# The first layer's first four modulation units: two channel tiles of shift and scale in each, and loads reordered to match

## What is computed

```python
c_act = silu(c)
for l in range(2):
    mod = c_act @ w_ada[l] + b_ada[l]                       # 6 * 1024 columns
    sh_mix, sc_mix, gt_mix, sh_mlp, sc_mlp, gt_mlp = split(mod, 6)
    h = rms_norm(x, g_pre_mix[l]) * (1 + sc_mix) + sh_mix
    y = mixer(h, w_in[l], ...)                              # u = h @ w_in first
    x = x + gt_mix * rms_norm(y, g_post_mix[l])
    ...
```

## Time and profile before

| | |
|---|---|
| three runs | 2279.96, 2281.36 (median), 2281.94 us |
| span of the profiled execution | 2274.4 us; its own run time is not among the numbers |
| mean granted TensorE clock | 0.994 of full speed |
| busy in the span | PE 2222.0 us (98%), DVE 1280.8 (56%), ACT 992.0 (44%), POOL 1131.6 (50%) |
| DMA, 0 to 80 us | 22.82 MB, mean 285 GB/s |
| DMA, whole span | 240.39 MB, mean 106 GB/s |

### The profile page before, as it was taken

How to read it: one execution, slowest core, us unless ns; L and a number is a source line. 1 busy time by engine, 2 the same in 40 slices (tenths; PEclk the granted TensorE clock), 3 DMA queues, 4 the chain that set the end, 5 groups by cost and what they waited for, 6 DMA issues and landing times.

```text
span 2274.4 us, 28727 instructions
## 1 busy us (share of the span) xinstructions
PE 2222.0 (98%) x10450; PEld 1749.5 (77%) x10450; DVE 1280.8 (56%) x2061; ACT 992.0 (44%) x1630; POOL 1131.6 (50%) x596
## 2 busy tenths in 40 slices
PE   8999999999999999999999999999999999999998
PEld 5886667788888878766778888887767688888886
DVE  4999847863546699984365122157776653221222
ACT  4368543333232335875344223244666653331323
POOL 2698833554444639876374344463422244444442
PEclk9999999999999999999999999999999999999999
DMA  8432205354646323221122323232222122333332
GB/s 319 138 98 71 65 29 172 120 185 157 231 166 217 96 77 94 75 84 38 56 84 86 99 93 101 87 108 72 82 57 65 47 92 94 103 92 97 97 99 86
DMA packets 206662, 240.39 MB, mean 106 GB/s; under 512 B 9762, under 2 KB 172378, under 8 KB 206554
## 3 DMA queue, kind: packets, MB, share of 16 engines
q1 hardware_dynamic: 205990, 238.76, 32.9%
q10 hardware_dynamic: 564, 0.21, 0.0%
HBM read 236.84 MB, written 2.10 MB: 105 GB/s over the span
## 4 chain that ended last, share of the span: by engine, by line
PE 52%; DVE 3%; POOL 2%; issue 2%; ACT 1%; DMA 0%; DVEq 0%; POOLq 0%; ACTq 0%; SPq 0%
PE product L2508 16%; PE product L2510 15%; PE product L2509 15%; DVE side L1888 1%; PE side L3076 1%; POOL ring_low L950 1%; PE product L3111 1%; POOL slot_f L981 1%; PE side L3096 1%; POOL slot_f L1003 1%; PE product L2881 1%; PE side L2865 0%; PE side L3023 0%; DVE slot_f L1888 0%; ACT sqt L1436 0%
## 5 line engine op out<-in xcount | busy, mean ns | idle before, releaser
L950 POOL TENSOR_TENSOR ring_low<-ring_f,ring_high 128x1024 fp32r<-128x1024 f32 (+1 forms) x349 | 845.6, 2427 | 1029.2 <-ACT ring_high L1076 1028.8
L2508 PE MATMUL product<-slot_r,ring_high 128*128 128x512 f32 (+1 forms) x2536 | 1007.1, 397 | 13.5 <-ACT slot_f L1282 4.0
L2510 PE MATMUL product<-slot_r,ring_high 128*128 128x512 f32 (+1 forms) x2536 | 989.3, 390 | 0.0
L2509 PE MATMUL product<-slot_r,ring_low 128*128 128x512 f32 (+1 forms) x2536 | 988.3, 390 | 0.0
L1076 ACT ACTIVATE ring_high<-ring_f 128x1024 fp32r<-128x1024 f32 (+1 forms) x349 | 367.8, 1056 | 697.9 <-DMA ring_f<-in_w_ff 326.0
L2508 PEld LDWEIGHTS product<-slot_r,ring_high 128*128 128x128 f32 (+1 forms) x2536 | 475.9, 188 | 146.4 <-issue 35.5
L2510 PEld LDWEIGHTS product<-slot_r,ring_high 128*128 128x128 f32 (+1 forms) x2536 | 475.9, 188 | 101.5
L2509 PEld LDWEIGHTS product<-slot_r,ring_low 128*128 128x128 f32 (+1 forms) x2536 | 476.4, 188 | 97.0 <-issue 1.4
L1845 DVE SCALAR_TENSOR_TENSOR va<-product,sqt 128x512 f32<-128x512 f32 x96 | 66.3, 692 | 332.9 <-ACT sqt L1154 331.6
L1888 DVE SCALAR_TENSOR_TENSOR side<-slot_f,cols,side 128x512 f32<-128x512 f32 x322 | 214.8, 747 | 0.0
L1865 DVE TENSOR_TENSOR slot_f<-product,slot_f 128x512 f32<-128x512 f32 x64 | 44.2, 691 | 161.6 <-PE product L2510 161.6
(11 more groups left out here) (325 smaller groups left out, 2164.8 us busy)
## 6 DMA issues: line engine op xcount, KB each, us to landing
ring_f<-in_w_ff SPq DMA_DIRECT2D x128, 512.0 KB, 3.8
slot_f<-in_w_ada SPq DMA_DIRECT2D x48, 1024.0 KB, 7.4
ring_f<-in_w_in SPq DMA_DIRECT2D x96, 512.0 KB, 3.9
ring_f<-in_w_out SPq DMA_DIRECT2D x40, 512.0 KB, 3.4
ring_f<-in_w_up SPq DMA_DIRECT2D x32, 512.0 KB, 3.7
ring_f<-in_w_down SPq DMA_DIRECT2D x32, 512.0 KB, 3.6
slot_f<-in_x SPq DMA_DIRECT2D x4, 512.0 KB, 5.0
ring_f<-in_w_v SPq DMA_DIRECT2D x4, 512.0 KB, 3.5
```

The lines of the kernel that those rows point to most:

```text
L950: pool.tensor_tensor(whole(ring_low[:, s, :, :], n), whole(ring_f[:, s, :, :], n), whole(ring_high[:, s, :, :], n).bitcast(F32), ALU.subtr ...
L2508: pe.matmul(out_ap, high, rhs_high, start=start, stop=False)
L2509: pe.matmul(out_ap, low, rhs_high, start=False, stop=False)
L2510: return pe.matmul(out_ap, high, rhs_low, start=False, stop=stop)
```

## The change

Each of the first four units now holds two tiles' worth of both kinds: unit u has shift and scale of tiles 2u and 2u + 1, 256 columns each, and the units are taken in the order 0, 1, 2, 3. A half of a unit is loaded as two pieces of 512 KB with 1 KB rows. On TensorE only unit 0 is summed ahead of the quad, with the parameter columns between its halves; units 1, 2 and 3 are summed ahead of k = 1, 3 and 5 and turned to columns between m = 1 and m = 2 of these k. VectorE and ScalarE go by pairs of tiles. Four calls of `keep_busy` with 5 products in all become one of 2.

```diff
-FIRST_UNITS = (0, 2, 1, 3)
+FIRST_UNITS = (0, 1, 2, 3)
+FIRST_PART = T // 2
...
             def load_first(unit):
                 for b in range(2):
...
+                    for part in range(2):
+                        at = part * D + unit * FIRST_PART
+                        sp.dma_start(ada_raw(FIRST_RAW[unit], b)[:, :, part * FIRST_PART:(part + 1) * FIRST_PART],
+                                     rows_of(w["w_ada"][0, rows_b, at:at + FIRST_PART])).then_inc(first_loaded[unit][b].sem, 16)
...
-                        for k in {0: (1,), 1: (2,), 2: (3,)}.get(n, ()):
+                        for k in {1: (1, 2), 3: (3,)}.get(n, ()):
                             load_first(FIRST_UNITS[k])
...
                 whole_unit(4, 0)
-                if l == 0:
-                    wait(sp, place, root_ready, 1)
-                whole_unit(5)
                 for p in range(1, 4):
                     load_pair(LAYER, I_GLU + 4 * p, w_in, 0, 3 * D + p * CW)
+                    if l == 0 and p == 1:
+                        wait(sp, place, root_ready, 1)
+                        whole_unit(5)
...
+                    for k in range(ADA_FIRST):
+                        first_rows_out(k)
+                        if k % 2 == 0:
+                            ahead.upto(place, k + 2)
+                        for t in (2 * k, 2 * k + 1):
+                            wait(act, place, hv_ready, t + 1)
+                            act.activation(tile_r(SA, t), va[:, t % 2, :], ACT.Identity,
+                                           bias=shift[:, t:t + 1]).then_inc(hh_ready.sem, 1)
+                    ahead.upto(place, EARLY)
...
+                for k in range(ADA_FIRST):
+                    next_columns(k)
+                    value(2 * k)
+                    value(2 * k + 1)
+                    low(2 * k)
+                    low(2 * k + 1)
...
+                    def next_columns(k):
+
+                        wait(dve, place, ada_cols, k + 1)
+                        c, n = 2 * k, 2 * k + 2
+                        moves, gains = first_columns(k)[:, 0:2], first_columns(k)[:, 2:4]
+                        steps.did(dve.tensor_tensor(gains, gains, cols[:, V_BADA + NT + c:V_BADA + NT + n], ALU.add))
+                        steps.did(dve.tensor_tensor(shift[:, c:n], moves, cols[:, V_BADA + c:V_BADA + n], ALU.add))
+                        steps.wait(steps.n - 1)
+                        steps.did(dve.scalar_tensor_tensor(scale[:, c:n], gains, 1.0, cols[:, V_GPREM + c:V_GPREM + n],
...
-                    wait(pe, Place(), first_loaded[unit][b], 16)
+                    wait(pe, Place(), first_loaded[unit][b], 16 * 2)
...
+            def next_columns(k, m):
+
+                if k in (1, 3, 5) and m == 2:
+                    first_columns_out(k // 2 + 1)
...
                     pe.wait_ge(c_act.sem, 1)
-                    first_sums(0)
+                    wait(pe, place, x_ready, 5)
+                    first_sums(0, lambda: params_columns(place, 0))
                     wait(pe, place, r_small, 1)
                     spread(PM[2], inv_cols[:, 0:BLK]).then_inc(r_ready.sem, 1)
-                    wait(pe, place, x_ready, 5)
-                    params_columns(place, 0)
                     first_columns_out(0)
-                    keep_busy(PM[0], 1)
-                    first_sums(1, lambda: keep_busy(PM[0], 1))
-                    first_columns_out(1)
                     keep_busy(PM[0], 2)
...
-                    if l == 0 and k == 3:
-                        first_sums(2)
-                        first_sums(3)
-                    if l == 0 and k == 4:
-                        keep_busy(PM[3], 1)
+                    if l == 0 and k in (1, 3, 5):
+                        first_sums(k // 2 + 1)
```

More of the change, by code:

```diff
@@ L781, in load_first @@
                 for b in range(2):
-                    src = w["w_ada"][0, b * 4 * P:(b + 1) * 4 * P, unit_cols(unit)]
-                    sp.dma_start(ada_raw(FIRST_RAW[unit], b), rows_of(src)).then_inc(first_loaded[unit][b].sem, 16)
+                    rows_b = slice(b * 4 * P, (b + 1) * 4 * P)
+                    if unit >= ADA_FIRST:
+                        sp.dma_start(ada_raw(FIRST_RAW[unit], b),
+                                     rows_of(w["w_ada"][0, rows_b, unit_cols(unit)])).then_inc(first_loaded[unit][b].sem, 16)
+                        continue
+                    for part in range(2):
+                        at = part * D + unit * FIRST_PART
+                        sp.dma_start(ada_raw(FIRST_RAW[unit], b)[:, :, part * FIRST_PART:(part + 1) * FIRST_PART],
+                                     rows_of(w["w_ada"][0, rows_b, at:at + FIRST_PART])).then_inc(first_loaded[unit][b].sem, 16)
             sp.dma_start(c_rows, w["c"][0].rearrange("(t p) -> t p", p=P)).then_inc(c_loaded.sem, 16)
@@ L1128, in output_stats, with split_high @@
                 deviation(place, x_sums, D, x_root, BLK)
-            def split_high(place, n, ahead, move=None, value=lambda t: va[:, t % 2, :], begin=None):
+            def split_high(place, n, ahead, move=None, value=lambda t: va[:, t % 2, :]):
                 for t in range(NT):
-                    if begin is not None and t == BLK:
-                        begin()
-                    if t == (0 if begin is None else BLK):
+                    if t == 0:
                         ahead.upto(place, AHEAD + 1)
@@ L1219, in _ @@
                 ahead = Ahead(LAYER, AHEAD if l else 0)
[L1220 to L1223, removed]
                 if l:
@@ L1703, in refine, with normalise @@
                 inverse_root(v, q, r, y, signal)
-            def normalise(place, gain, move, last_gains):
+            def normalise(place, gain, move, next_columns):
                 wait(dve, place, r_ready, 1)
@@ L1966, in _ @@
                 if l == 0:
[L1967 to L1970, removed]
+                    def next_columns(k):
[6 more added lines that the diff above has]
+                        steps.did(dve.scalar_tensor_tensor(scale[:, c:n], gains, 1.0, cols[:, V_GPREM + c:V_GPREM + n],
                                                            ALU.add, ALU.mult))
                         steps.wait()
[L1974 to L1985, removed]
+                    normalise(place, lambda t: scale[:, t:t + 1], lambda t: shift[:, t:t + 1], next_columns)
                 steps.did(dve.memset(region_f[:, SD:SE].rearrange("p (t c) -> p t c", t=NT)[:, :, 0:CONV_C - 1], 0.0))
@@ L2735, in _ @@
                     if p == 0:
-                        use_quad(place, LAYER, I_GLU, O_GLU, (SA, SB_), h, last_columns if l == 0 else lambda k, m: None)
+                        use_quad(place, LAYER, I_GLU, O_GLU, (SA, SB_), h, next_columns if l == 0 else lambda k, m: None)
                     else:
```

## The result

| | before | after |
|---|---|---|
| median of the timed runs | 2281.65 us (6 runs, 2278.45 to 2282.41) | 2289.56 us (6 runs, 2284.74 to 2292.11) |
| span of the profiled execution | 2274.4 us | 2290.3 us |
| product behind the first columns of unit 4 starts | 57.27 us | 66.08 us |
| TensorE busy, 20 to 100 us | 78.19 us | 69.63 us |

The ratio is 1.0035, with a 95% interval of 1.0024 to 1.0046: the changed kernel is slower by some 8 us. The forecast was a loss of 2.9 us, in a range that ended at 2288.0; the direction was right, the size was not. The opening can be compared.

A forecast was written before the change was run, and what follows sets the result against it. TensorE, hardly idle behind the opening, bounds the kernel. A 5.8 us earlier start is spent in three rounds (quad ends 57.4), then 1.9 waiting for unit 4: 2.9 us later, 2284.3 us, range 2279.0 to 2288.0.

The forecast's parts named there:

- k = 0 to k = 2: First round in the quad: 2.76 + 1.8 + 1.38 + 3.89 = 9.83 us, plus 0.3 waiting for the second chunk's low part.
- the mark: Start of the product behind unit 4's columns: forecast 60.1 us against 57.27 before, 2.9 us later.
- The head start: Opening on TensorE: the first quad product starts 5.8 us earlier, since unit 0 alone carries shift and scale for tiles 0 and 1.
- with 3.98 the first product starts at 22.13: Ahead of the quad: 3.98 us from the columns' start at 18.15 to the first product needing VectorE's low tile.
- the 3.89 for each round: Inside the quad: 3.89 us from the columns' start to the next even k's first product, read from the kernel before.
- ready at 21.4: GpSimd's first low part, ahead of k = 0: starts at 19.05, takes 2.35 us, ready at 21.4.
- ends at 23.8: GpSimd's low part of the second chunk: ends at 23.8, m = 2 of k = 0 asks at 23.5, costing 0.3 us.
- Rival 1: Clock falls in TensorE's idle holes, losing 1.9 us: one fall gives 2286.2, two 2288.1; chance 0.10.
- holes of 1.6: TensorE idles some 1.6 us in each of three rounds, ahead of k = 2, 4 and 6, waiting for VectorE's low tile.
- rival 2: Loads of w_ada pieces come late: at 2.0 us a piece units 0, 1 and 3 are late, near 2288.8; chance 0.08.
- rival 4: Delay absorbed behind the opening: TensorE's 2.0 us of idle in 120 to 180 come back, giving 2282.3; chance 0.12.
- 7 us above that span, which I leave as it is: Whole kernel before: timed median 2281.36 us stands 7 us above the profiled span of 2274.4; this gap was left unchanged.

The follow-up runs named there:

- experiment 7: Changed kernel with value tile 0 in PSUM, sums of units 2 and 3 one step earlier, columns of units 1 to 3 moved: 2280.04 us, 0.9995 of the kernel before.
- Experiments 1: Changed kernel, but ScalarE makes the high part of chunk 1 (and 3) behind the rounding of the pair's tiles: 2292.04 us in one run.
- experiment 2: Changed kernel with even value tiles in PSUM instead of SBUF and all four units' sums on side 0: 2288.6 us, 1.004 of the kernel before.
- experiment 5: Change unedited, timed again: 2290.72 us, 1.0039 of the kernel before; kernel before profiled a second time: span 2281.4 us.
- experiment 4: Changed kernel with the first four units loaded in 1 MB pieces with 2 KB rows, shift and scale for other channels: 2290.71 us, 1.0052 of the kernel before.
- experiment 6: Changed kernel with even value tiles in PSUM plus short keep-busy products in TensorE's holes: 2285.14 us, 1.0018 of the kernel before.

## Why the prediction was wrong

By its own terms, in the first profile of the change:

| term | forecast | measured | off by |
|---|---|---|---|
| first quad product | 22.13 | 24.45 | +2.3 |
| k = 0 to k = 2 | 9.83 + 0.3 | 34.47 - 24.45 = 10.0 | -0.1 |
| k = 2 to k = 4 | 9.83 | 46.36 - 34.47 = 11.9 | +2.1 |
| k = 4 to k = 6 | 9.83 | 57.97 - 46.36 = 11.6 | +1.8 |
| k = 6 to the mark | 60.1 - 51.9 = 8.2 | 66.08 - 57.97 = 8.1 | -0.1 |
| the mark | 60.1 | 66.08 | +6.0 |

- **The mechanism held.** The head start is spent in the pairs' rounds, TensorE waits for the low tile ahead of k = 2, 4 and 6 and for unit 4 behind the quad, and where nothing was held and the clock kept up, a round is 10.0 (34.47 - 24.45), against 9.83. The edit that puts work into exactly these waits (experiment 7) takes all of the loss away.
- **The step that failed: "with 3.98 the first product starts at 22.13", and the 3.89 for each round.** Both were taken from a kernel in which a low tile met at most the last 0.15 us of a low part of GpSimd: 0.75 a tile. The change makes ScalarE do two chunks' high parts in a row, right before a pair's rounding, and so puts two of GpSimd's low parts, 4.7 us, over the pair's low tiles. The forecast timed the low parts ("ready at 21.4", "ends at 23.8") and set them against TensorE's need alone, never against the low tile that falls between. Cost: 2.1 and 1.8 us over 0.75 in the first profile; in the second the 1.8 ahead of k = 4, and in the first round 0.6 of waiting for the second low part. Experiments 1 and 2 show what does it: with GpSimd's second part elsewhere the same tile takes 0.75, and with one operand in PSUM it takes 0.75 beside the part.
- The rule was there to be read. The Trainium skill, "SBUF — State Buffer", section "Who interferes with whom", says that a VectorE instruction with two SBUF inputs contends with a GpSimd instruction that reads SBUF, that whoever issues first has the shared ports for its whole duration, and that one with at most one SBUF input, outside the 2-port perf modes, does not contend. The runs agree on each count: 2.44 and 2.89 against 0.75 with two SBUF inputs; 0.76 for tile 0 and 2.83 instead of 2.35 for GpSimd where VectorE was first (experiment 5); and the value tiles with PSUM at 0.74.
- **Rival 1 had 0.10 and came true as part of it.** It decides "from the first" fall; there were two in one profile (some 1.5 in k = 4, 4.53 against 2.99, and one more behind the mark), and a longer one in the other. The argument against it, that two thirds of each round are full products, was made for holes of 1.6; the fall ahead of the mark stands behind the hole that the held tile had stretched to 3.1. But such a hole is neither needed nor enough: experiment 2 shows a fall with no idle above 1.5 us ahead of it, and experiment 4 none in k = 4 behind an idle of 3.12. By the terms of the first profile the two holds alone (2.1 and 1.8) give 2288.2, just past the range, and the fall in k = 4 alone 2285.8; measured, the kernel in which TensorE waits for no held tile and the clock keeps 2.4 GHz up to 100 us stands at 2285.14 (experiment 6), 0.8 from the forecast of 2284.3.
- Right: the round's shape; the head start lost; unit 4 waited for (1.5, forecast 1.9); every load in time (rival 2 falls: at 348 to 350 GB/s 512 KB take 1.50 us, the upper price that was chosen, and experiment 4 shows that the faster pieces win nothing); nothing seen to be absorbed later (rival 4: behind the mark the eight profiles of the change and its edits take 2221.7 to 2224.5 us with no order by the mark, though with this spread a part of its 2.0 could not be seen).
- "7 us above that span, which I leave as it is" was safe: the profile of before was quick by some 6 us, all of it behind the opening, and the sum never used that part.

## What to carry to other kernels

When a change brings two engines' work together that stood apart, list for the new overlap who reads what from where, and don't carry a duration over from a trace in which they hardly met. Moving one operand into PSUM, or the GpSimd work by a pair, is a cheap test of such a hold. When work must go inside a loop with a long chain across engines, count the chain from the end of the producer and place the producer one step earlier; filling the hole with dummy products keeps the clock, but must be shorter than the hole.

## Not expected of the hardware

- The hold is decided by a tenth of a microsecond or less: the same program held tile 0 in one execution (both engines start at 21.51) and tile 1 in the next (21.44 and 21.61), and the addition at 1652.71 took 0.29 or 2.51 us with both engines starting within 0.01 us. Some 2 us of a single profile are such luck.
- Behind one and the same hole of 3.1 us the granted clock can fall for a shorter or a longer time, or not at all: k = 4 took 4.53 us (0.67 from 45 to 50 us), 5.42 (0.50 throughout), and 2.99 in experiment 4 (1.00).
- Pieces of `w_ada` of 512 KB with rows of 1 KB move at 348 to 350 GB/s where loads with pieces of 1 MB and rows of 2 KB move at 375 to 388; whether the size or the row does it is not shown.
